# Hyena transforms at odd frequencies, with filters and inverse folded in halves and the value projection placed between their steps

## The chip, the cores and the metric

One core of a Trainium2 chip runs the whole program in a single launch. The metric is the device time in microseconds; three runs of the kernel before stand behind the median. The engines are named as in the profile: PE (TensorE matmuls), PEld (its weight loads), DVE (VectorE), ACT (ScalarE), POOL (GpSimd), SP (which issues the weight transfers).

## The reference

Two transformer blocks on 512 tokens of width 1024, all in float32. The change lies in the first mixer of the first block: two long convolutions over 512 positions, for 512 channels, with filters that a small network makes.

```python
def hyena_filters(L, ...):            # z: 33 features of each of the L times
    h = sin(freq[0] * (z @ w1 + b1)); h = sin(freq[1] * (h @ w2 + b2))
    h = (h @ w3).reshape(L, 2, ORDER, HY_W) * exp(-t * deltas)
    h_fwd, h_bwd = h[:, 0], h[:, 1]
    k2 = concatenate([h_fwd, zeros, h_bwd[1:][::-1]])     # length 2L
    return rfft(k2, axis=0)
def long_conv(z, kf, bias):
    zf = rfft(z, n=2 * L, axis=1)
    return irfft(zf * kf, n=2 * L, axis=1)[:, :L] + z * bias
def hyena_mixer(u, short_w, kf, bias):
    v, x1, x2 = split(dwconv3(u, short_w), 3)
    z = x1 * long_conv(v, kf[:, 0], bias[0])
    return x2 * long_conv(z, kf[:, 1], bias[1])
```

Beside it stand the input projection (`h @ w_in`, whose first 1536 columns feed this mixer and others the attention's queries, keys and values), neighbourhood attention, cross attention, two gated feed-forward networks and a second block. None of these is computed differently after the change.

## The kernel before

A float32 product is made of three passes: each operand is kept as a pair (hi, lo) of float32r tiles, and `mm` issues hi by hi, hi by lo and lo by hi, lines 370 to 372, each a matmul with a weight load of its own. The weights stream in as chunks of [128, 1024]: SP loads one into `raw` (4 buffers), ACT writes its hi part (line 299, `ws_h`), DVE subtracts to get the lo part (line 307, `ws_l`), into one of 3 split buffers. `chunk_act` and `chunk_dve` stand at fixed places in the two engines' programs and split up to two chunks beyond the one that PE is about to use, as far as buffers are free by then. All engines run their instructions in the order in which the functions issue them; semaphores alone tie them together. That order is written by hand: `hyena_pe`, `hyena_act`, `hyena_dve`, `hyena_pool`, then the same four for attention (`na_...`) and so on.

The Hyena part goes like this on PE. A tile `("hy", m)` is 8 blocks of the projection, 24 matmuls of 512 columns and one chunk; 12 of them make v, x1 and x2. A tile `("s", o, tt, i)` is 3 matmuls, and makes the sum (i = 0) or the difference (i = 1) of the forward and backward filter of order o at 128 times; DVE multiplies it by the decay (line 758), ACT makes the hi part (644), DVE the lo part (739, `mg_l`). `filters_pe(o)` transforms the four time tiles at frequencies 0 to 511 in four chunks (96 matmuls), and 12 more matmuls make the frequency 512 that an even transform also has. `long_conv_pe(o, src)` transposes the data (16 transposes), transforms it (96 matmuls, four chunks, results `zr`, `zi`), waits for the products with the filter, and transforms back (96 matmuls of 512 columns, four chunks, into four banks `("y", o, j)`). The products take four DVE multiplications from PSUM for each 128 frequencies (line 888), a subtraction and an addition on POOL (908), the hi parts on ACT (705, 708) and the lo parts on DVE (875). The whole for o = 0, then eight `s` tiles in a row (`HY2`), then the whole for o = 1. The banks come from a ring of seven. The eighth holds the totals of the norms.

In the hand-written order ACT and DVE finish a tile three steps behind its issue (`finish(HY1[n - 3])`), and DVE does a whole tile at once: scale, wait for ACT's middle tap, two side taps of the width-3 convolution (lines 748, 850, 853). After `("hy", 6)` DVE and ACT normalise the 16 meta tokens in 8 pairs of small operations each. `na_pe` starts with the value projection, `("V", m)`, four tiles of 24 matmuls, then the first query and key tiles, then the first scores.

## Time and profile before

| what | before |
|---|---|
| median of 3 runs | 2037.41 us (2033.86 to 2037.97) |
| the profiled execution | 2034.22 us, of which the span from first to last instruction is 2032.4 us |
| PE busy | 1885.5 us (93%), 9041 matmuls |
| DVE busy | 1013.8 us (50%) |
| ACT busy | 752.2 us (37%) |
| POOL busy | 273.2 us (13%) |
| mean granted TensorE clock | 0.962 |
| first matmul of the projection, last inverse matmul of o = 1 | 22.63 us, 270.66 us |
| first scores of the attention | 308.71 us |

Times inside the program are counted from the start of the span. A matmul's busy time in the profile is its latency: matmuls overlap, so the distance between the starts of two that follow each other (the pitch) is what one costs on PE. Idle time on PE is shown in brackets, with what ended it.

### The profile page before, as it was taken

How to read it: one execution, taken by the hardware profiler on the slowest of the kernel's cores; microseconds unless marked ns; L12 is line 12 of the kernel's file. 1: busy time of each engine (PE TensorE's matmuls, PEld its weight loads, DVE VectorE, ACT ScalarE, POOL GpSimd, SP SyncE). 2: the span in 40 equal slices, each digit the busy share in tenths (PEclk: the TensorE clock that was granted, in tenths of full speed). 3: DMA queues.
4: the chain of work that ended last, by engine and by line, in shares of the span. 5: the costliest groups of instructions: out<-in, count | busy, mean ns of one | idle time of the engine just before them, and what ended most of it. 6: DMA issues, size and time to landing. Idle time of an engine off the chain costs nothing. (4 is left out here: it accounts for less than half of the span.)

```text
span 2032.4 us, 22399 instructions
## 1 busy us (share of the span) xinstructions
PE 1885.5 (93%) x9041; PEld 1504.5 (74%) x9041; DVE 1013.8 (50%) x1510; ACT 752.2 (37%) x1248; POOL 273.2 (13%) x227
## 2 busy tenths in 40 slices
PE   5898999999999989889999999878967989999997
PEld 4776777678888877777888778766745668888886
DVE  6657554444354364445777722445454544444422
ACT  4343324432333443343434422325355533232221
POOL 1001200011211330042111100500000011111100
PEclk9998999999999999989999999888977999999998
DMA  5122232223223342122332232221220122222221
GB/s 177 63 94 73 83 114 84 73 82 106 83 93 102 137 145 73 34 70 78 99 104 83 83 104 94 93 84 42 90 73 16 36 82 84 94 93 94 94 93 52
DMA packets 49831, 175.35 MB, mean 86 GB/s; under 512 B 5883, under 2 KB 6523, under 8 KB 49601
## 3 DMA queue, kind: packets, MB, share of 16 engines
q1 hardware_dynamic: 45792, 160.41, 24.0%
q0 software_dynamic: 3936, 13.51, 1.9%
q8 instruction: 72, 1.18, 0.2%
q14 instruction: 31, 0.25, 0.0%
HBM read 169.70 MB, written 4.19 MB: 86 GB/s over the span
## 5 line engine op out<-in xcount | busy, mean ns | idle before, releaser
L307 DVE TENSOR_TENSOR ws_l<-raw,ws_h 128x1024 fp32r<-128x1024 f32 x297 | 401.1, 1354 | 587.2 <-ACT ws_h L299 586.7
L370 PE MATMUL ps<-h_h,ws_h 128*128 128x512 f32 (+1 forms) x1448 | 584.1, 403 | 42.7 <-DVE ws_l L307 23.3
L371 PE MATMUL ps<-h_l,ws_h 128*128 128x512 f32 (+1 forms) x1448 | 572.0, 395 | 0.0
L372 PE MATMUL ps<-h_h,ws_l 128*128 128x512 f32 (+1 forms) x1448 | 571.2, 395 | 0.0
L299 ACT ACTIVATE ws_h<-raw 128x1024 fp32r<-128x1024 f32 x297 | 312.2, 1055 | 489.9 <-PE ps L372 489.5
L370 PEld LDWEIGHTS ps<-h_h,ws_h 128*128 128x128 f32 x1448 | 278.3, 192 | 118.2 <-issue 22.9
L372 PEld LDWEIGHTS ps<-h_h,ws_l 128*128 128x128 f32 x1448 | 278.2, 192 | 61.6
L371 PEld LDWEIGHTS ps<-h_l,ws_h 128*128 128x128 f32 x1448 | 279.4, 193 | 59.0 <-issue 0.5
L370 PE MATMUL ps<-G_h,ws_h 128*128 128x512 f32 x352 | 139.8, 397 | 3.0 <-DVE ws_l L307 3.0
L372 PE MATMUL ps<-G_h,ws_l 128*128 128x512 f32 x352 | 139.7, 397 | 0.0
L371 PE MATMUL ps<-G_l,ws_h 128*128 128x512 f32 x352 | 139.6, 397 | 0.0
L414 POOL TENSOR_TENSOR sums<-sums,tmp 128x512 f32<-128x512 f32 (+2 forms) x48 | 53.7, 1119 | 494.3 <-ACT tmp L410 490.3
L370 PEld LDWEIGHTS ps<-G_h,ws_h 128*128 128x128 f32 x352 | 66.3, 188 | 19.7 <-DVE ws_l L307 3.5
L370 PE MATMUL ps<-mg_h,ws_h 128*128 128x512 f32 x200 | 79.5, 397 | 0.0
L371 PE MATMUL ps<-mg_l,ws_h 128*128 128x512 f32 x200 | 79.3, 396 | 0.0
L372 PE MATMUL ps<-mg_h,ws_l 128*128 128x512 f32 x200 | 79.2, 396 | 0.0
L371 PEld LDWEIGHTS ps<-G_l,ws_h 128*128 128x128 f32 x352 | 66.4, 189 | 16.3
L372 PEld LDWEIGHTS ps<-G_h,ws_l 128*128 128x128 f32 x352 | 66.4, 188 | 16.3
L370 PE MATMUL ps<-ya_h,ws_h 128*128 128x512 f32 (+1 forms) x160 | 58.1, 363 | 8.8 <-DVE ws_l L307 7.4
L1766 POOL TENSOR_TENSOR tmp<-tmp,tmp 128x512 f32<-128x512 f32 x22 | 35.2, 1600 | 210.7 <-DVE tmp L853 210.7
L1890 POOL TENSOR_TENSOR tmp<-tmp,tmp 128x512 f32<-128x512 f32 x22 | 28.7, 1306 | 225.4 <-ACT tmp L1839 190.3
L371 PE MATMUL ps<-ya_l,ws_h 128*128 128x512 f32 (+1 forms) x160 | 57.4, 359 | 0.0
(409 smaller groups left out, 2471.7 us busy)
## 6 DMA issues: line engine op xcount, KB each, us to landing
raw<-in_ffn_up SPq DMA_DIRECT2D x88, 512.0 KB, 3.4
raw<-in_w_merge SPq DMA_DIRECT2D x36, 512.0 KB, 3.4
raw<-in_ffn_down SPq DMA_DIRECT2D x22, 512.0 KB, 3.5
raw<-in_w_down SPq DMA_DIRECT2D x22, 512.0 KB, 3.4
raw<-in_fwd SPq DMA_DIRECT2D x16, 512.0 KB, 3.5
raw<-in_w_hy SPq DMA_DIRECT2D x12, 512.0 KB, 3.5
raw<-in_w_sc SPq DMA_DIRECT2D x12, 512.0 KB, 3.4
raw<-in_inv SPq DMA_DIRECT2D x8, 512.0 KB, 3.5
```

The lines of the kernel that those rows point to most:

```text
L299: act.e.activation(wsp[n % NSPLIT].hi, raw[n % NRAW][:], ACT.Copy).then_inc(*hi_made.says(("hi", n)))
L307: dve.e.tensor_tensor(w.lo, raw[n % NRAW][:], w.hi, ALU.subtract).then_inc(*lo_made.says(("lo", n)))
L370: pe.e.matmul(o, a.hi, b.hi, start=start, stop=False, skip_group_check=True)
L371: pe.e.matmul(o, a.hi, b.lo, start=False, stop=False, skip_group_check=True)
L372: return pe.e.matmul(o, a.lo, b.hi, start=False, stop=stop, skip_group_check=True)
L414: line.e.tensor_tensor(acc[:, 0:W], acc[:, 0:W], T[place.get(("sq", v, m), 0)][:, 0:W], ALU.add).then_inc(*sig.says(("added", v, m), ("gon ...
L1766: pool.e.tensor_tensor(u, u, v, ALU.mult).then_inc(*pool_part.says(("glu", i), ("gone", ("u", i, 1))))
L1890: pool.e.tensor_tensor(u, u, v, ALU.mult).then_inc(*pool_part.says(("glu2", i), ("gone", ("n8", i, 1))))
```

## The change

- The long convolutions are transformed at the 512 odd frequencies (2k + 1) of a doubled grid, not at 0 to 512. There is no separate last frequency, and no row 0 to mask (`row0`, `notrow0`, `KA` rows 8 and the DVE step on line 861 go).
- The 512 times are reordered, even ones first, in the filters' inputs and in the transposes (which now read the data with a step of two). Frequency k and 511 - k then have the same even part and the opposite odd part, up to sign. A filter transform `("F", o, q)` makes 128 + 128 frequencies from an even half and an odd half, 8 products of 3 matmuls, one chunk `fold`: 24 matmuls for 256 frequencies. ACT copies the even results out of PSUM, DVE makes sum and difference, four operations, into `KA` (`KA1` for o = 1).
- The data are transformed as before, in tiles `("Z", o, q, up)`, 24 matmuls and a chunk each. The products are written by DVE into `scr`, which lies in the space of `mg`.
- POOL now makes F and G of each Z tile (2 operations) and then, for each pair of Z tiles, the sums and differences of the two halves (4 operations, `("U", o, q)`), 8 for each q, 32 in all where there were 16. ACT and DVE split them into hi and lo as before.
- The inverse `("I", o)` works with 256 columns: even and odd times of the output are separate halves of a bank, two chunks, 96 matmuls of 256 columns.
- The order is one list, `HY_STEPS`, that PE, ACT and DVE all follow (`follow_steps`). Both orders' filters are made first, between the `hy` tiles. The last two `hy` tiles stand between the last Z tile of o = 0 and its inverse, and the four V tiles stand in the same way around the second convolution. DVE and ACT take up a tile one step after its issue; side taps and lo parts of the `s` tiles come one step later still.
- The banks come from one ring of eight. The meta tokens are normalised in one squaring, one reduction and two multiplications. The attention's biases of all four first heads are loaded only when the last inverse is done, since `y01` and `sums` now hold parts of the Hyena work.

On PE, at the head of the inverse of o = 0. Before (names: `ws` a weight chunk, `ya` the transposed data, `mg` the products KY), where the last matmuls of the transform of the data come right ahead:

```order
L371 MATMUL ps<-ya_l,ws_h 128x512
L372 MATMUL ps<-ya_h,ws_l 128x512
L370 MATMUL ps<-ws_h,mg_h 128x512
L371 MATMUL ps<-ws_l,mg_h 128x512
L372 MATMUL ps<-ws_h,mg_l 128x512
```

And after, where the last three matmuls of `("hy", 11)` come right ahead:

```order
L372 MATMUL ps<-h_h,ws_h 128x512
L373 MATMUL ps<-h_l,ws_h 128x512
L374 MATMUL ps<-h_h,ws_l 128x512
L372 MATMUL ps<-ws_h,mg_h 128x256
L373 MATMUL ps<-ws_l,mg_h 128x256
L374 MATMUL ps<-ws_h,mg_l 128x256
```

The number of inverse matmuls stays at 96 for each order. Their width goes from 512 to 256.

On POOL, the first Hyena operations. Before (behind the last sum for the meta tokens; all on four kept and two passing temporaries):

```order
L414 TENSOR_TENSOR sums<-sums,tmp_71 128x16
L908 TENSOR_TENSOR tmp_71<-tmp_71,tmp_75 128x512
L908 TENSOR_TENSOR tmp_72<-tmp_72,tmp_76 128x512
L908 TENSOR_TENSOR tmp_73<-tmp_73,tmp_75 128x512
L908 TENSOR_TENSOR tmp_74<-tmp_74,tmp_76 128x512
```

After (the four products of two Z tiles, then the folds into what ACT and DVE split):

```order
L888 TENSOR_TENSOR tmp_71<-scr_0_170,scr_1_171 128x512
L888 TENSOR_TENSOR tmp_72<-scr_2_172,scr_3_173 128x512
L888 TENSOR_TENSOR tmp_73<-scr_4_174,scr_5_175 128x512
L888 TENSOR_TENSOR tmp_74<-scr_6_176,scr_7_177 128x512
L888 TENSOR_TENSOR y_68<-tmp_71,tmp_73 128x512
L888 TENSOR_TENSOR tmp_71<-tmp_71,tmp_73 128x512
L888 TENSOR_TENSOR tmp_73<-tmp_72,tmp_74 128x512
L888 TENSOR_TENSOR tmp_72<-tmp_72,tmp_74 128x512
```

Four operations now stand for what were four, and four more follow them before ACT may start.

On DVE, around the split of the first chunk that the filter transform uses. Before (`ws_l` rows are the split chunks, 758 the decay, 739 the lo part, 748 the scaling of a `hy` tile):

```order
L748 TENSOR_TENSOR tmp_76<-ps,rh 128x512
L739 TENSOR_TENSOR mg_l<-tmp_74,mg_h 128x512
L850 SCALAR_TENSOR_TENSOR x_82<-tmp_76,par,x_82 128x511
L853 SCALAR_TENSOR_TENSOR x_82<-tmp_76,par,x_82 128x511
L758 TENSOR_TENSOR tmp_71<-ps,dec 128x512
L307 TENSOR_TENSOR ws_l<-raw_53,ws_h 128x1024
L307 TENSOR_TENSOR ws_l<-raw_54,ws_h 128x1024
```

And after (776 the decay, 842 the lo part, 770 the scaling, 873 and 876 the side taps):

```order
L842 TENSOR_TENSOR mg_l<-tmp_74,mg_h 128x512
L776 TENSOR_TENSOR tmp_71<-ps,dec 128x512
L873 SCALAR_TENSOR_TENSOR x<-tmp_75,par,x 128x511
L876 SCALAR_TENSOR_TENSOR x<-tmp_75,par,x 128x511
L776 TENSOR_TENSOR tmp_72<-ps,dec 128x512
L842 TENSOR_TENSOR mg_l<-tmp_71,mg_h 128x512
L776 TENSOR_TENSOR tmp_73<-ps,dec 128x512
L842 TENSOR_TENSOR mg_l<-tmp_72,mg_h 128x512
L309 TENSOR_TENSOR ws_l<-raw_56,ws_h 128x1024
L309 TENSOR_TENSOR ws_l<-raw_53,ws_h 128x1024
L776 TENSOR_TENSOR tmp_74<-ps,dec 128x512
```

The first of the two splits that follow each other is the chunk that `("F", 0, 0)` needs. It stands behind the operations of both groups of `s` tiles of o = 0.

The diff, cut to its core:

```diff
     def hyena_pe():
+        main = Ring(place, range(8))
...
+    HY_STEPS = ([("hy", m) for m in range(4)] + s_tiles(0, (0, 1)) + [("hy", 4)] + s_tiles(0, (2, 3)) + [
+        ("hy", 5), ("F", 0, 0), ("hy", 6), ("F", 0, 1)] + s_tiles(1, (0, 1)) + [("hy", 7)] + s_tiles(1, (2, 3)) + [
+        ("hy", 8), ("F", 1, 0), ("zT", 0), ("F", 1, 1), ("hy", 9), ("Z", 0, 0, 0), ("Z", 0, 0, 1), ("Z", 0, 1, 0),
+        ("Z", 0, 1, 1), ("U", 0, 0), ("hy", 10), ("U", 0, 1), ("hy", 11), ("I", 0), ("V", 0), ("V", 1), ("zT", 1),
+        ("Z", 1, 0, 0), ("Z", 1, 0, 1), ("Z", 1, 1, 0), ("Z", 1, 1, 1), ("U", 1, 0), ("V", 2), ("U", 1, 1), ("V", 3),
+        ("I", 1)])
...
+        def F(o, q):
+            n = chunk_pe("fold")
+            w = wsp[n % NSPLIT]
+            for odd in range(2):
+                for c in range(2):
+                    b = bank(("F", o, q, c, odd), main)
+                    for i in range(2):
+                        tt = 2 * odd + i
+                        pe.wait_ge(("sd", o, tt, c))
+                        last = mm(b, w[:, (4 * c + tt) * 128:(4 * c + tt + 1) * 128], (S_, D_)[c][:, tt, :], i == 0, i == 1)
+                last.then_inc(*products.says(("done", ("F", o, q, odd)), over(n) if odd else None))
...
+        def I(o):
+            ys = [bank(("y", o, j), main) for j in range(4)]
+            for q in range(2):
+                n = chunk_pe("inv")
+                w = wsp[n % NSPLIT]
+                for i in range(4):
+                    pe.wait_ge(("KY", o, 4 * q + i))
+                    for j, y in enumerate(ys):
+                        at = 256 * (i // 2)
+                        k = mm(y[:, at:at + 256], KY[:, 4 * q + i, j * 128:(j + 1) * 128], w[:, i * 256:(i + 1) * 256],
+                               q == 0 and i == 0, q == 1 and i % 2 == 1)
+                k.then_inc(*products.says(over(n), ("done", ("y", o, q))))
...
+    def follow_steps(chunk, begun, first, second):
+        for n, t in enumerate(HY_STEPS):
+            if t[0] in ("hy", "F", "Z", "V") or t[0] == "s" and t[2:] == (0, 0):
+                chunk()
+            elif t[0] == "I":
+                chunk()
+                chunk()
+            begun(t)
+            if n == 2:
+                first(HY_STEPS[0])
+            if n > 1:
+                first(HY_STEPS[n - 1])
+                second(HY_STEPS[n - 2])
...
     def hyena_pool():
+            for q in range(2):
+                for up in range(2):
+                    for i, (name, op) in enumerate((("F", ALU.subtract), ("G", ALU.add))):
+                        pool.wait_ge((a,) + t, (b,) + t, old)
+                        add(o, T[s][:, 0:L], scr[q][4 * up + 2 * i], scr[q][4 * up + 2 * i + 1], op, (name,) + t)
+                add(o, T[s][:, 0:L], at(Fa), at(Fb), ALU.add, u + (0,))
+                add(o, at(Fa), at(Fa), at(Fb), ALU.subtract, u + (2,))
+                add(o, at(Fb), at(Ga), at(Gb), ALU.subtract, u + (1,))
+                add(o, at(Ga), at(Ga), at(Gb), ALU.add, u + (3,), ("gone", Gb))
...
     def na_pe():
-        for m in range(4):
-            tile(bank(("V", m), vr), vblocks, 8, hk, ("V", m))
...
     def na_pool():
-            ready = ("neg", 4 * (hd // 2 - 2) + 3, hd % 2) if hd > 3 else ("sum", "meta") if hd == 1 else (
-                "done", ("y", 1, 3)) if hd > 1 else None
+            ready = ("neg", 4 * (hd // 2 - 2) + 3, hd % 2) if hd > 3 else ("done", ("y", 1, 1))
```

## Rows read from the trace of the kernel before

**Rows 1.** The page: span, busy time, granted TensorE clock in 40 slices
```profile
span 2032.4 us, 22399 instructions
...
PE 1885.5 (93%) x9041; PEld 1504.5 (74%) x9041; DVE 1013.8 (50%) x1510; ACT 752.2 (37%) x1248; POOL 273.2 (13%) x227
...
PEclk9998999999999999989999999888977999999998
```

**Rows 2.** Busy time by stretch: length, then busy and count by engine, clock, DMA
```profile
39.10:84.00 44.90, 42.62 (x184) 34.02 (x182) 30.52 (x47) 18.16 (x35) 2.33 (x7) 1.00 0.29 95
84.00:111.00 27.00, 22.71 (x88) 17.39 (x88) 21.55 (x31) 11.17 (x16) 0.00 (x0) 0.94 0.24 78
111.00:182.00 71.00, 70.27 (x310) 56.65 (x309) 39.71 (x47) 25.00 (x35) 12.51 (x8) 1.00 0.26 86
182.00:200.00 18.00, 12.90 (x38) 8.69 (x37) 15.50 (x24) 5.91 (x9) 0.00 (x0) 0.72 0.13 43
...
270.90:308.70 37.80, 35.59 (x161) 28.59 (x160) 20.85 (x27) 10.57 (x14) 1.07 (x2) 1.00 0.30 98
```

**Rows 3.** Waits of PE from 39 to 295 us: total, times, longest
```profile
PE ps L370 <- DVE x L809: 5.1, 4, 1.6
PE ps L370 <- DVE ws_l L307: 4.1, 2, 2.4
```

**Rows 4.** Timeline of PE: start, duration; 512 and 256 columns at both clocks
```profile
195.25 0.63 PE L371 MATMUL ps<-ws_l,HD_h 128*128 128x512 f32 x1
195.68 0.63 PE L372 MATMUL ps<-ws_h,HD_l 128*128 128x512 f32 x1
...
270.43 0.40 PE L371 MATMUL ps<-ws_l,mg_h 128*128 128x512 f32 x1
270.66 0.40 PE L372 MATMUL ps<-ws_h,mg_l 128*128 128x512 f32 x1
...
702.12 0.41 PE L370 MATMUL ps<-ya_h,ws_h 128*128 128x256 f32 x1
702.33 0.41 PE L371 MATMUL ps<-ya_l,ws_h 128*128 128x256 f32 x1
...
705.11 0.28 PE L372 MATMUL ps<-ya_h,ws_l 128*128 128x256 f32 x1
...
708.96 0.28 PE L372 MATMUL ps<-ya_h,ws_l 128*128 128x256 f32 x1
```

**Rows 5.** Timeline of DVE: the reciprocal, and two operations back to back
```profile
41.63 3.35 DVE L434 RECIPROCAL rh<-rh 128x512 f32<-128x512 f32 x1 [0.78 <-ACT rh L429]
...
94.65 0.68 DVE L739 TENSOR_TENSOR mg_l<-tmp,mg_h 128x512 fp32r<-128x512 f32 x1
95.25 0.68 DVE L758 TENSOR_TENSOR tmp<-ps,dec 128x512 f32<-128x512 f32 x1
```

**Rows 6.** Groups to 300 us, by shape: busy, mean ns, idle before
```profile
L299 ACT ACTIVATE ws_h<-raw 128x1024 fp32r<-128x1024 f32 x45 | 46.9, 1055 | 45.9 <-PE ps L372 45.8
...
L888 DVE TENSOR_TENSOR tmp<-ps,KA 128x512 f32<-128x512 f32 x32 | 19.8, 680 | 9.7 <-PE ps L372 9.7
...
L853 DVE SCALAR_TENSOR_TENSOR x<-tmp,par,x 128x511 f32<-128x511 f32 x12 | 9.0, 751 | 0.4
```

**Rows 7.** Timelines of DVE and POOL where both work, and DVE's splits
```profile
152.01 2.58 DVE L875 TENSOR_TENSOR mg_l<-tmp,mg_h 128x512 fp32r<-128x512 f32 x2
154.52 1.21 DVE L307 TENSOR_TENSOR ws_l<-raw,ws_h 128x1024 fp32r<-128x1024 f32 x1
...
717.29 2.28 DVE L307 TENSOR_TENSOR ws_l<-raw,ws_h 128x1024 fp32r<-128x1024 f32 x1
...
151.05 3.00 POOL L908 TENSOR_TENSOR tmp<-tmp,tmp 128x512 f32<-128x512 f32 x2 [2.07 <-DVE tmp L888]
...
722.02 10.32 POOL L414 TENSOR_TENSOR sums<-sums,sq 128x512 f32<-128x512 f32 x5
```

**Rows 8.** Timeline of PE: after the transposes, and the first scores
```profile
138.14 0.47 PE L370 MATMUL ps<-ya_h,ws_h 128*128 128x512 f32 x1 [0.73 <-DVE ya_l L868]
...
308.71 0.38 PE L1027 MATMUL ps<-mg_h 64*128 64x256 f32 x2 [0.52 <-DVE mg_l L1161]
```

More of the change, by code:

```diff
@@ new lines, in hy, with s @@
+            if m == 5:
+                total("meta", 16, bank(("sum", "meta"), main), 8, False)
+        chunk = {}
+        def s(o, tt, i):
+            if (tt, i) == (0, 0):
+                chunk["w3"] = chunk_pe("w3")
+            n = chunk["w3"]
+            b = bank(("s", o, tt, i), main)
+            pe.wait_ge(("H", i))
+            mm(b, (HS, HD)[i][:, tt * 128:(tt + 1) * 128], wsp[n % NSPLIT][:, o * 512:(o + 1) * 512], True, True).then_inc(
+                *products.says(("done", ("s", o, tt, i)), over(n) if (tt, i) == (3, 1) else None))
@@ new lines, in Z @@
+            for c in range(2):
+                b = bank(("Z", o, q, up, c), main)
+                for k in range(4):
+                    pe.wait_ge(("zt", o, k))
+                    i = mm(b, w[:, (4 * c + k) * 128:(4 * c + k + 1) * 128], zt[:, k, :], k == 0, k == 3)
+            i.then_inc(*products.says(over(n), ("done", ("Z", o, q, up))))
+        def I(o):
[10 more added lines that the diff above has]
+                k.then_inc(*products.says(over(n), ("done", ("y", o, q))))
@@ new lines, in V @@
+        def V(m):
+            tile(bank(("V", m), main), vblocks, 8, hk, ("V", m))
+        do = dict(hy=hy, s=s, F=F, zT=zT, Z=Z, I=I, V=V, U=lambda o, q: None)
+        for t in HY_STEPS:
+            do[t[0]](*t[1:])
+    def follow_steps(chunk, begun, first, second):
[11 more added lines that the diff above has]
+                second(HY_STEPS[n - 2])
+        first(HY_STEPS[-1])
+        second(HY_STEPS[-2])
+        second(HY_STEPS[-1])
@@ L719, in hyena_dve @@
+        follow_steps(chunk_act, begun, first, lambda t: None)
     def hyena_dve():
@@ new lines, in second @@
+        def second(t):
+            if t[0] == "hy":
+                m = t[1]
+                conv_sides(vx(m), t_slot(t)[:, 0:L], lambda q: P("hy_short", q * 12 + m), ("middle", t), ("side", t),
+                           ("v", 0, m), ("gone", t))
+            elif t[0] == "s":
+                _, o, tt, i = t
+                dst = (S_, D_)[i][:, tt, :]
+                dve.wait_ge(("f hi", t))
+                dve.e.tensor_tensor(dst.lo, t_slot(t)[:, 0:L], dst.hi, ALU.subtract).then_inc(
+                    *dve_part.says(("sd",) + t[1:], ("gone", t)))
@@ L824, in sine @@
+        follow_steps(chunk_dve, begun, first, second)
     def sine(b, n, i, bias, freq, slots):
@@ L1035, in V @@
                 pe.wait_ge(*(("scaled", ("V", m)) for m in range(4)))
-                transposes(b, [t_slot(("V", m))[:, 128 * tt:128 * tt + 128] for m in range(4)], ("done", ("Vt", tt)),
-                           *((("gone", ("V", m)) for m in range(4)) if tt == 3 else ()))
+                transposes(b, [vt(m)[:, 128 * tt:128 * tt + 128] for m in range(4)], ("done", ("Vt", tt)))
         def turn(t):
@@ L1147, in scaled @@
             return u
-        for m in range(4):
-            vblocks.next(8)
-            scaled(("V", m), kept)
         def project(p):
```

459 lines of the change are left out of this document (178 added, 281 removed).

## The prediction

> **What bounds the kernel now.** I read the page first: PE is busy 93% of a span of 2032.4 us, DVE 50%, POOL 13% [rows 1]. So time goes down either by fewer or shorter matmuls, or where PE waits. Then the stretches of the Hyena part, one row each, for the count of matmuls and the clock [rows 2], the list of PE's waits there [rows 3], and PE's timeline for what one matmul costs [rows 4]. At full clock a 512-column matmul starts 0.23 us after the one before (270.43 to 270.66; over 111 to 182 us, 294 of them besides 16 transposes, it comes to 0.233). At the low level of the clock, 1.2 GHz, it is 0.43 (195.25 to 195.68). A 256-column one takes 0.117 (33 of them from 705.11 to 708.96) and 0.21 at the low level (702.12 to 702.33) [rows 4]. So the busy time of a matmul, 0.40 or 0.28, is not what it costs.
>
> The two good stretches, such as 111 to 182 us, hold no waits worth naming. The bad ones are 84 to 111 us, 88 matmuls in 27.0 us where 88 x 0.233 = 20.5 would do, and 182 to 200, 38 in 18.0 us where 8.9 would do, at a clock of 0.72 [rows 2]. There the `s` tiles follow each other, and for each PE needs 0.7 us but DVE 1.2 (a decay and a lo part at a pitch of 0.60 [rows 5]). PE's own waits there are short (line 809, 1.6 us at most [rows 3]), and the halved clock behind them costs about as much again. With 2.3 us at 84 us and 0.73 at each data transform [rows 8], the Hyena part loses 6.5 + 9.1 + 2.3 + 1.5 = 19.4 us to waits and low clock after the first tiles.
>
> **The change on PE.** Filters: before 2 x (96 + 12) = 216 matmuls, after 4 F tiles of 24, so 120 fewer, 120 x 0.233 = 28.0 us. Inverse: 192 matmuls go from 0.233 to 0.117 [rows 4]: 22.3 us. Everything else on PE stays: 288 for `hy`, 48 for `s`, 192 for the data, 96 for V, 32 transposes. The transposes read the data with a step of two; no row shows that, and I bound it between nothing and a doubling of the 32 x 0.1 us that they take, so 0 to 3 us, and take 0, as only the 128-column weight load is strided. PE's work falls by 50.3 us. With all 19.4 us of loss gone too, 69.7 us would be the whole gain. What remains is which waits the new order has.
>
> **New waits, in order of time.** I lay DVE's list against PE's, with these prices: a split 1.14 (1.21 less the overlap), a PSUM or lo operation 0.60, the two side taps 1.5 [rows 5 to 7], a split on ACT 1.06 [rows 6].
>
> (1) The first filter transform. PE is free to begin it at 39.1 + 4 `hy` tiles x 5.6 + 8 `s` tiles x 0.7 = 67.1 us. DVE does the reciprocal first (3.35 us [rows 5], now behind one split, ending at 47.2) and then, before the split of the `fold` chunk is done: 5 scalings 3.0, 5 pairs of taps 7.9, 7 decays 4.2, 6 lo parts 3.6, 3 splits 3.4, some 1.0 of waiting for ACT: 23.1, hence 70.3 to 70.8. A wait of 3.6 us, and 0.9 more for the last lo part of the difference. 4.5 us, of which a lower clock behind it may cost 2 more (a clock of 0.94 over 27 us [rows 2] is 1.6).
>
> (2) The second group, eight `s` tiles with one `hy` tile between, then `F` for o = 1: the same list, but with an F and a `hy` tile of slack ahead, where DVE needs 4.1 and 3.2 us of PE's 5.6. I find it 1 us late.
>
> (3) The two stretches of Z tiles. Here DVE has per tile a split and four multiplications, 3.5 us of 5.6, and POOL 16 operations for each order. What one costs is between 1.3 (the shortest of its kind, estimated as 3.00 / 2 less the wait inside) and 2.06 (10.32 / 5, where DVE works beside it); 3.00 / 2 = 1.50 is the same operation in the same place [rows 7], and I take that. From the start of the first Z tile, the last 14 begin at +15.5 us (second Z tile done at 11.2, its products 1.6 to 2.4, a wait for DVE's split) and end at +36.5, then ACT's hi 0.6 and DVE's lo parts until about +39.5. PE needs the second half of the products at +39.1: four Z tiles 22.3, two `hy` tiles (or V2 and V3) 11.2, first half of the inverse 5.6. So the cover of 39.1 us is just enough. The products are asked for one by one over 5.6 us, so what is a little late costs little. At 2.06 the end is +47, 4 us late or more. At the same place DVE's split of the second inverse chunk is queued behind ACT's middle tap and four lo parts. I take 1.5 us for o = 0 and 1.0 for o = 1.
>
> What the row shows of DVE beside POOL: two lo parts take 2.58 us while POOL adds, 1.29 each, against a pitch of 0.60 alone, and a split takes 2.28 beside POOL's work and 1.21 alone [rows 5, 7]. I use these where they overlap. The Trainium skill, page "SBUF — State Buffer", section "Who interferes with whom", says that a DVE instruction with two SBUF inputs and a GpSimd instruction that reads SBUF block each other wholly, whoever starts first. By that rule six of DVE's operations and six of POOL's would stand strictly in turn, 13.7 us, and the second inverse chunk would be split at the moment when PE asks for it instead of 4 us before; the sum would rise by 0 to 2 us for each order. The 2.58 us agree with the rule, and so do the multiplications from PSUM, whose mean is 0.68 over all 32 [rows 6], as that of the decays alone [rows 5].
>
> (4) Data of o = 1: V0 and V1 (11.2 us) cover the 5.4 us in which DVE finishes the convolution; behind the transposes a wait of 1 us as before (0.73 [rows 8]). For o = 0 the F tile and a `hy` tile cover it: none.
>
> (5) The attention. Before, V's 22.3 us covered DVE's end of the convolution, and PE waited 0.52 us for the first scores [rows 8]. Now the query and key tiles, 11.2 us, come at once, and DVE has 8.6 us of work (12 operations) first, then two splits, two scalings and two lo parts. I reckon 2 us, 1.5 more than before. The biases, asked for only now, have 12 us to land. The other stages are unchanged, with the same waits.
>
> Chunks: 8 fewer, so DVE and ACT each lose 8 splits, off the path, and the transfers are not scarce.
>
> **The sum.** Work 50.3, old losses 19.4, new ones 4.5 + 2 + 1 + 1.5 + 1 + 1 + 1.5 = 12.5, which gives 57 us less: 2034.2 to 1977 for a profiled execution. The profiled one before stands 3.2 us below the median of its runs, 2037.41. I put the median after between the two readings: 1979.
>
> **Rivals.** (A) No new wait lasts: 3 us in all, gain 67, 1970. For it speaks that the first wait hangs on one reckoning of DVE's list. (B) POOL is the bound of both Z stretches: at 2.06 us an operation, with DVE's splits queued behind it, PE waits 4 to 8 us for each order and the clock falls behind each wait, 5 us more for each. Gain 57 less 17 to 24, so 1996 to 2003. For it speaks that DVE and POOL would each be busy over three quarters of a stretch where before POOL was busy for 12.5 of 71 us [rows 2]; against it, the 1.50 in the same place. (C) The other side, the clock. The new order has a short wait ahead of nearly every step, and if the engine is held at 1.2 GHz a 512-column matmul costs 0.43 instead of 0.233. Before, it fell so after waits of about 1.6 and 1.6 us with 6 matmuls between (0.72 over 18 us [rows 2, 3]). The gain of 57 us is gone when some 290 of the 720 matmuls of 512 columns that are left run so, 125 us at the low level, since each costs 0.197 more; with 400 of them the time is 1979 + 79 = 2058. Against it: wherever PE had 0.7 us of wait or less between tiles the clock stayed at 1.00 (111 to 182 us [rows 2]). (D) The halves don't shorten the inverse, if 256 columns were held up by strided output or by the weight load, 22 us less gain, 2001. The matmuls at 705 us had a weight load each and ran at 0.117 [rows 4], so this is nearly shut out.
>
> **Chances.** Forecast 0.60, A 0.15, B 0.18, C 0.02, D and the like 0.05. The range is from 1966 (A, and a low reading) to 1999 (most of B); C and the rest are left out. The likeliest case alone: 1970 to 1988. About 0.2%, 4 us, is what the measurement can tell from no change. Faster 0.97, same 0.01, slower 0.02.
>
> **What would show it.** PE: 120 matmuls fewer; inverse matmuls at a pitch of 0.12; a bracket of 3 to 4 us before the first F tile, named after DVE's split, and small ones at the second inverse chunk of each order; the first scores at about 252 us instead of 308.7. POOL: 32 additions with a mean near 1.5. Wrong it would be by a mean over 2, by brackets of many us named after POOL's or ACT's hi of the products, or by a clock under 0.9 in the Hyena part.

## The result

| what | before | after |
|---|---|---|
| median | 2035.63 us (4 runs, 2032.52 to 2037.97) | 1969.93 us (4 runs, 1965.65 to 1978.72) |
| ratio | | 0.9684, 95% interval 0.9646 to 0.9721 |
| profiled execution | 2034.22 us, span 2032.4 us | 1965.65 us, span 1963.9 us |
| first projection matmul to first scores | 286.08 us (22.63 to 308.71) | 225.49 us (21.79 to 247.28) |
| from the first scores to the end of the span | 1723.7 us | 1716.6 us |

A second profile of the same kernel, with five timed rounds, gave 1977.15 us against 2040.8, ratio 0.9684 (0.9661 to 0.9706). The change is worth 3.2%, and the prediction of 1979 us (1966 to 1999) was right in sign and nearly in size: 9 us too high beside the first median. Between the two profiles of the table, 60.6 us come from the stretch that the change rewrites and 7.1 from behind it. The second figure is no firm one: in the ten profiles of the kernel after and of the versions of it below, bank3 left out, the time from the first scores to the end lies anywhere from 1716.0 us (hy_early) to 1733.2 us (hy_before_f).

The page of the kernel after, to be held against [rows 1]:

```profile
span 1963.9 us, 22095 instructions
PE 1831.5 (93%) x8921; PEld 1468.3 (75%) x8921; DVE 1015.5 (52%) x1504; ACT 734.2 (37%) x1216; POOL 295.7 (15%) x236
PEclk9999999999999899999999999889987989999998
```

There are 120 matmuls fewer, as reckoned. PE's busy share is 93% as before: its busy time fell by 54.0 us, its idle time from 146.9 to 132.4. Next, PE's timeline in the kernel after: every start in the Hyena part and at the attention's head with a wait of over 0.4 us, behind the first tiles (it answers [rows 3, 8]), with the transposes of o = 1.

```profile
69.21 0.74 PE L372 MATMUL ps<-mg_h,ws_h 128*128 128x512 f32 x1 [3.58 <-DVE ws_l L309]
106.45 0.50 PE L372 MATMUL ps<-mg_h,ws_h 128*128 128x512 f32 x1 [1.87 <-DVE ws_l L309]
182.92 2.07 PE L393 MATMUL ps<-ident,x 128*128 128x128 f32 x16
186.24 0.47 PE L372 MATMUL ps<-ya_h,ws_h 128*128 128x512 f32 x1 [1.25 <-DVE ya_l L791]
233.60 0.51 PE L372 MATMUL ps<-h_h,ws_h 128*128 128x512 f32 x1 [2.16 <-DVE x L807]
247.28 0.39 PE L1027 MATMUL ps<-mg_h 64*128 64x256 f32 x2 [0.52 <-DVE mg_l L1154]
```

The two rows that answer [rows 2] around the filters, the window of each order's POOL work, and the first inverse on PE (its first two and its last matmul, then the next tile's first):

```profile
67.00:90.00 23.00, 20.79 (x82) 16.64 (x83) 14.86 (x21) 10.47 (x15) 0.00 (x0) 0.93 0.35 115
90.00:115.00 25.00, 23.13 (x98) 18.55 (x97) 21.03 (x32) 11.33 (x17) 0.00 (x0) 0.93 0.25 85
...
136.30:165.10 28.80, 28.80 (x146) 24.09 (x145) 25.50 (x26) 8.50 (x12) 25.27 (x16) 1.00 0.23 73
195.80:224.50 28.70, 28.70 (x144) 23.95 (x143) 24.55 (x25) 8.23 (x11) 25.17 (x16) 1.00 0.27 89
```

```profile
160.35 0.28 PE L372 MATMUL ps<-ws_h,mg_h 128*128 128x256 f32 x1
...
171.60 0.28 PE L374 MATMUL ps<-ws_h,mg_l 128*128 128x256 f32 x1
171.72 0.39 PE L372 MATMUL ps<-h_h,ws_h 128*128 128x512 f32 x1
```

The 96 matmuls of the inverse run from 160.35 to 171.72, 0.118 each, without one wait between them. In the first window beside POOL, PE is busy without a break, DVE for 25.5 us of 28.8 and POOL for 25.3: three engines are nearly full at once, and PE waits for neither of the others.

### The profile page after: what moved, and what is told of

The parts are those of the page before. It is cut to its first block and busy times, and to the rows that moved or that the text cites. A ratio compares the mean times of both kernels' runs of the same rounds, so it can differ in the third digit from the quotient of the medians.

```text
span 1963.9 us, 22095 instructions
## 1 busy us (share of the span) xinstructions
PE 1831.5 (93%) x8921; PEld 1468.3 (75%) x8921; DVE 1015.5 (52%) x1504; ACT 734.2 (37%) x1216; POOL 295.7 (15%) x236
## 5 line engine op out<-in xcount | busy, mean ns | idle before, releaser
L309 DVE TENSOR_TENSOR ws_l<-raw,ws_h 128x1024 fp32r<-128x1024 f32 x289 | 393.1, 1364 | 577.1 <-ACT ws_h L301 576.8
L301 ACT ACTIVATE ws_h<-raw 128x1024 fp32r<-128x1024 f32 x289 | 303.9, 1055 | 504.9 <-PE ps L374 504.6
L373 PEld LDWEIGHTS ps<-h_l,ws_h 128*128 128x128 f32 x1448 | 279.0, 193 | 59.1 <-issue 0.5
L416 POOL TENSOR_TENSOR sums<-sums,tmp 128x512 f32<-128x512 f32 (+1 forms) x41 | 51.6, 1259 | 455.8 <-ACT tmp L412 453.0
L374 PEld LDWEIGHTS ps<-G_h,ws_l 128*128 128x128 f32 x352 | 66.0, 187 | 16.3
L372 PE MATMUL ps<-mg_h,ws_h 128*128 128x512 f32 x160 | 64.7, 405 | 5.4 <-DVE ws_l L309 5.4
L373 PE MATMUL ps<-mg_l,ws_h 128*128 128x512 f32 x160 | 64.5, 403 | 0.0
L374 PE MATMUL ps<-mg_h,ws_l 128*128 128x512 f32 x160 | 64.4, 402 | 0.0
L374 PE MATMUL ps<-ya_h,ws_l 128*128 128x512 f32 (+1 forms) x160 | 57.5, 359 | 0.0
```

What stands on the lines that cost most here:

```text
L301: act.e.activation(wsp[n % NSPLIT].hi, raw[n % NRAW][:], ACT.Copy).then_inc(*hi_made.says(("hi", n)))
L309: dve.e.tensor_tensor(w.lo, raw[n % NRAW][:], w.hi, ALU.subtract).then_inc(*lo_made.says(("lo", n)))
L372: pe.e.matmul(o, a.hi, b.hi, start=start, stop=False, skip_group_check=True)
L373: pe.e.matmul(o, a.hi, b.lo, start=False, stop=False, skip_group_check=True)
L374: return pe.e.matmul(o, a.lo, b.hi, start=False, stop=stop, skip_group_check=True)
L416: line.e.tensor_tensor(acc[:, 0:W], acc[:, 0:W], T[place.get(("sq", v, m), 0)][:, 0:W], ALU.add).then_inc(*sig.says(("added", v, m), ("gon ...
```

## Experiments

Each is told by what it tells apart. "The distance" is the time from the first projection matmul to the first scores in its profile, 225.49 us in the kernel after. Its second profile has 227.48, with a clock of 0.94 in one window of 30 us (210 to 240) where the first has 1.00, behind the same wait of 2.16 us: some 2 us are noise of the clock. The stretch from the first projection matmul to the first F tile, the same program in all versions that leave it alone, takes from 47.4 to 48.5 us (pool_more), so another 1 us of the distance is noise.

### The terms of PE's work: fold_more and inv512

Thirty matmuls more in each F tile (54, where there are 24):

```diff
-                        last = mm(b, w[...], (S_, D_)[c][:, tt, :], i == 0, i == 1)
+                        for again in range(2 if c or i else 3):
+                            last = mm(b, wt, st, i == 0 and again == 0, i == 1)
```

> The kernel after with 30 matmuls more in each of the four F tiles (54 instead of 24: as many as the unfolded filters had, 216 in all; some of them are accumulated several times, so the filters' spectra are wrong). It measures the term 'filters, 120 x 0.233 = 28.0 us'. Theory 1: TensorE alone sets the time: 28 us more than the kernel after. Theory 2: part of what the fold saved went into the waits for the splits around it: DVE catches up during the longer F tiles, the waits of 1.9 us before F of the second order and the low clock behind go, and it costs only 22 to 26 us more.

```profile
70.84 0.50 PE L372 MATMUL ps<-mg_h,ws_h 128*128 128x512 f32 x1 [3.59 <-DVE ws_l L309]
...
85.09 0.40 PE L372 MATMUL ps<-h_h,ws_h 128*128 128x512 f32 x1
```

The F tile takes 14.25 us here, from its first start to that of the `hy` tile behind it, and 7.26 in the kernel after; the four tiles together take 28.0 us more, as reckoned. The distance is 253.76 us, 28.3 more; the ratio to before is 0.9835 (0.9804 to 0.9867). Theory 1. The waits of 3.59 and 1.88 us before the F tiles stand unchanged, so longer F tiles do not help DVE to be in time.

The inverse with 512 columns instead of 256:

```diff
-                        at = 256 * (i // 2)
-                        k = mm(y[:, at:at + 256], KY[...], w[:, i * 256:(i + 1) * 256], ...)
+                        at = 512 * (i // 2)
+                        k = mm(y, KY[...], w[:, at:at + 512], ...)
```

> The kernel after with the same 192 inverse matmuls at 512 columns each instead of 256 (the inverse is then computed wrongly: each takes both halves of the chunk). It measures the term 'inverse, 22.3 us' of the sum. Theory 1: the inverse is bound by TensorE alone, each matmul goes from 0.117 to 0.233, 22.3 us more than the kernel after: ratio to it 1.011. Theory 2: the halves hung on the products of POOL and DVE (no slack), so that with 512 columns part of the 22.3 us only fills what would have been waits: 10 to 20 us more.

```profile
162.50 0.40 PE L372 MATMUL ps<-ws_h,mg_h 128*128 128x512 f32 x1
...
184.90 0.40 PE L372 MATMUL ps<-h_h,ws_h 128*128 128x512 f32 x1
```

The first inverse takes 22.40 us from its first start to the next tile's, where the kernel after has 11.37, and the second grows by as much: 22.1 us for both, against 22.3 reckoned. The distance is 249.34 us, 23.9 more. The 1.8 us that it has beyond are 1.0 before the first F tile (noise, as said), a clock of 0.91 over 250 to 270 us (1.8), and against them a clock of 1.00 over 90 to 115 us where the kernel after has 0.93 (1.75 less, with a wait of 0.65 us for a lo part showing in its place). The ratio is 0.9813 (0.9783 to 0.9843). The listed waits are those of the kernel after to 0.01 us, so nothing of the 22 us had been bought with a wait for POOL or DVE. Theory 1 again.

### The work alone in the old order: old_order_less_work

```diff
-            for k in range(4):
+            for k in range(2):
...
-                    k = mm(y, KY[...], w[:, i * 512:(i + 1) * 512], ...)
+                    k = mm(y[:, 256 * i:256 * i + 256], KY[...], w[:, i * 512:i * 512 + 256], ...)
```

> The kernel before, in its order and on its banks, with the change's saving of matmuls alone: filter transforms with two of four time tiles each (102 matmuls instead of 216, 114 x 0.233 = 26.6 us) and inverse matmuls at 256 columns (192 x 0.116 = 22.3 us); half of the filters' times and half of the inverse's frequencies are left out, so the output is another. Theory 1: work alone, and the order gave the rest: 48.9 us less than the kernel before, waits as there. Theory 2: without the new order the saved work turns into waits for DVE's products and splits (the Z and U tiles stood apart), so 25 to 45 us less. The kernel after is 64 us less.

The distance is 245.92 us, 40.2 less than before's 286.08, where 48.9 us of work are gone. Ratio 0.9795 (0.9763 to 0.9828), 40.7 us by the medians. Theory 2: 8.7 us did not come, mostly turned into waits and low clock. Its timeline and windows of PE:

```profile
156.82 0.39 PE L370 MATMUL ps<-ws_h,mg_h 128*128 128x256 f32 x1 [2.61 <-DVE ws_l L307]
...
223.99 0.58 PE L370 MATMUL ps<-ws_h,mg_h 128*128 128x256 f32 x1 [2.56 <-DVE ws_l L307]
```

```profile
84.00:111.00 27.00, 22.13 (x85) 16.92 (x86) 21.49 (x31) 10.76 (x15) 0.00 (x0) 0.94 0.23 77
165.00:190.00 25.00, 19.75 (x64) 14.04 (x65) 19.77 (x30) 12.75 (x19) 0.00 (x0) 0.80 0.22 68
```

The first window is as bad as it was before [rows 2], and so is the row of `s` tiles in the second. In either inverse a new wait of 2.6 us has come: with halved matmuls PE asks for the next chunk earlier than DVE can split it. The kernel after does 1.4 us less work than this one and is 20.4 us shorter in the distance. 19 us are the order's, with all that belongs to it, and that is more than the order: this run still splits 44 chunks in the distance, where the kernel after splits 36, and the two new waits (5.2 us) stand in inverses that use four chunks each instead of two. The order with the old chunks, or the old order with the new ones, was not run, so how the 19 us divide is not shown.

### What the order covers: hy_early, v_after, pool_more

The last two `hy` tiles ahead of the Z tiles of o = 0:

```diff
-        ... ("hy", 9), ("Z", 0, 0, 0), ... ("Z", 0, 1, 1), ("U", 0, 0), ("hy", 10), ("U", 0, 1), ("hy", 11), ("I", 0),
+        ... ("hy", 9), ("hy", 10), ("hy", 11), ("Z", 0, 0, 0), ... ("Z", 0, 1, 1), ("U", 0, 0), ("U", 0, 1), ("I", 0),
```

> The kernel after with the last two hy tiles (11.2 us) ahead of the four Z tiles of o = 0, so that they no longer stand between these and the first inverse. Same work. It measures the slack of POOL's and DVE's chain at the first inverse. Theory 1: the last products are ready only 0.6 to 3 us before TensorE asks for them, so 8 to 10.6 us of wait appear in the first inverse. Theory 2: the chain's end is itself set by the order (POOL starts on the last products when DVE and the banks let it), so it moves forward with them and 0 to 5 us appear.

```profile
163.83 0.36 PE L372 MATMUL ps<-ws_h,mg_h 128*128 128x256 f32 x1 [3.70 <-DVE mg_l L825]
167.10 0.58 PE L372 MATMUL ps<-ws_h,mg_h 128*128 128x256 f32 x1 [0.81 <-DVE mg_l L825]
176.64 0.36 PE L372 MATMUL ps<-ws_h,mg_h 128*128 128x256 f32 x1 [3.20 <-DVE mg_l L825]
```

```profile
165.00:190.00 25.00, 20.99 (x118) 19.34 (x117) 14.37 (x16) 4.42 (x7) 9.58 (x6) 0.81 0.19 64
```

Taking 11.2 us of cover away brings 7.7 us of wait, a little under what theory 1 expected (8 to 10.6), and far over theory 2. So the chain had 3.5 us to spare, not nothing. The clock falls to 0.81 behind the waits, and the distance grows by 14.0 us, or 12.0 beside the second profile of the kernel after: 1.6 to 1.8 times the waits. The ratio is 0.9713 (0.9689 to 0.9737).

The V tiles behind the second inverse:

```diff
-        ("I", 0), ("V", 0), ("V", 1), ("zT", 1), ... ("U", 1, 0), ("V", 2), ("U", 1, 1), ("V", 3), ("I", 1)])
+        ("I", 0), ("zT", 1), ... ("U", 1, 0), ("U", 1, 1), ("I", 1), ("V", 0), ("V", 1), ("V", 2), ("V", 3)])
```

> The kernel after with the four V tiles of the value projection (22.4 us of TensorE work) put back behind the second inverse, where the kernel before had them. Theory 1, by DVE's and POOL's lists: V0 and V1 cover the 5.4 us in which DVE ends the first convolution, V2 and V3 give 11.2 of the 39 us that POOL and DVE need for the second order's products. Without them TensorE waits about 5 us at the data transposes of o = 1 and 8 to 11 us in the second inverse, and the 2.2 us before the first query tile go: 12 to 16 us later at the first scores than the kernel after (225.5 us from the first projection matmul), with a clock under 1.00 behind the waits. Theory 2: POOL runs far enough ahead, so only the 5 us come, less 2: 3 us later.

```profile
178.73 3.66 PE L393 MATMUL ps<-ident,x 128*128 128x128 f32 x16 [5.32 <-DVE x L813]
...
208.87 0.55 PE L372 MATMUL ps<-ws_h,mg_h 128*128 128x256 f32 x1 [3.30 <-DVE mg_l L825]
...
221.69 0.55 PE L372 MATMUL ps<-ws_h,mg_h 128*128 128x256 f32 x1 [3.88 <-DVE mg_l L825]
```

5.3 us at the transposes, 7.6 in the second inverse (a wait of 0.38 lies between the two shown), and the 2.2 before the first query tile are gone: 10.7 us of waits on balance, 16.3 us in the distance, with a clock of 0.86 in the two windows 165 to 190 us and 210 to 240 us. The ratio is 0.9753 (0.9728 to 0.9778). Theory 1, with a little less wait in the inverse than its 8 to 11; the placing of V between the steps is worth 14 to 16 us of the 65.

Each of POOL's additions for F and G twice:

```diff
+                        add(o, T[s][:, 0:L], scr[q][4 * up + 2 * i], scr[q][4 * up + 2 * i + 1], op, ("first", name) + t)
+                        pool.wait_ge(("first", name) + t)
                         add(o, T[s][:, 0:L], scr[q][4 * up + 2 * i], scr[q][4 * up + 2 * i + 1], op, (name,) + t)
```

> The kernel after with each addition of the filters' unfolding on POOL done twice (the same sum into the same place): 16 additions more for each order, 32 in all, of 1.3 us alone and 1.7 beside DVE. Theory 1 (POOL just fits into its cover, the forecast's place for rival B): those of them that stand in POOL's chain ahead of the last products, about half of the 16, at 1.3 to 1.7 us less the slack of 0.6 to 3, show as a wait in each inverse: 8 to 12 us for each order, 16 to 24 in all. Theory 2 (POOL is off the path by far, since it idles while TensorE does the next tile): under 5 us in all.

The expectation counts them wrongly: F and G make 8 additions for each order, so 8 were added for each, 16 in all, not 16 and 32. The waits are 6.06 and 0.38 us in the first inverse, 5.24 and 0.38 in the second:

```profile
173.02 0.55 PE L372 MATMUL ps<-ws_h,mg_h 128*128 128x256 f32 x1 [6.06 <-DVE mg_l L825]
...
240.59 0.55 PE L372 MATMUL ps<-ws_h,mg_h 128*128 128x256 f32 x1 [5.24 <-DVE mg_l L825]
```

```profile
165.00:190.00 25.00, 18.56 (x103) 16.45 (x102) 16.09 (x19) 7.16 (x9) 10.31 (x8) 0.86 0.24 84
240.00:260.00 20.00, 16.88 (x78) 14.69 (x79) 16.59 (x22) 7.33 (x11) 5.37 (x6) 0.76 0.37 116
```

The four waits make 12.1 us, under the 16 to 24 of theory 1, which had counted twice the additions, and far over the 5 of theory 2; the distance grows by 19.2 us, and the ratio is 0.975 (0.9722 to 0.9779). Theory 1: POOL stands right behind the path, and rival B named the right place. By the 3.5 us of hy_early, some four microseconds more of POOL for the first order would have made it the bound (an estimate).

### The waits before the filter transforms: hy_before_f, early_split, early_split_o0

First a `hy` tile more ahead of the F tiles of either order:

```diff
-        ("hy", 5), ("F", 0, 0), ("hy", 6), ("F", 0, 1)] + s_tiles(1, (0, 1)) + [("hy", 7)] + ...
+        ("hy", 5), ("hy", 6), ("F", 0, 0), ("hy", 7), ("F", 0, 1)] + s_tiles(1, (0, 1)) + [("hy", 8)] + ...
```

> The changed kernel with one more projection tile ahead of the first filter transform of each order (hy 6 before F of order 0, hy 9 before F of order 1), all else in the same order. Theory 1: the waits of 3.58 us at 69 us and of 1.87 us at 106 us come from DVE's list, which is late by the work of the s tiles, and 5.6 us more of PE's work cover them. Then both brackets go, with the stretch at the low clock behind each, and the time is 6 to 9 us below the changed kernel. Theory 2: DVE is the bound of this whole stretch (busy 25.3 of 27.9 us), and the waits only move to the tiles behind. Then the gain is under 3 us and brackets show up later, before the first Z tile.

```profile
70.22 0.47 PE L372 MATMUL ps<-h_h,ws_h 128*128 128x512 f32 x1 [3.69 <-DVE ws_l L309]
...
112.99 0.50 PE L372 MATMUL ps<-mg_h,ws_h 128*128 128x512 f32 x1 [1.86 <-DVE ws_l L309]
```

The wait of 3.6 us did not go, it moved to the `hy` tile that now stands there. The distance (226.99) and the ratio (0.968, 0.9656 to 0.9705) are those of the kernel after, so theory 2 has the gain right; but no new wait shows up further on, the old two stay. So it is not a wait for the filters: it is the next chunk, whatever it holds. In the kernel after, ACT and DVE do this at the second place:

```profile
104.10 1.99 ACT L301 ACTIVATE ws_h<-raw 128x1024 fp32r<-128x1024 f32 x2
```

```profile
103.44 0.68 DVE L842 TENSOR_TENSOR mg_l<-tmp,mg_h 128x512 fp32r<-128x512 f32 x1
105.17 2.36 DVE L309 TENSOR_TENSOR ws_l<-raw,ws_h 128x1024 fp32r<-128x1024 f32 x2 [1.05 <-ACT ws_h L301]
```

Two chunks are split back to back at the end of DVE's list for the eight `s` tiles. DVE is not busy right before them: it idles 1.05 us here, and 1.04 at the first place (67.93 us), until ACT has split its half, and ACT has that behind the hi part of an `s` tile, which waits for DVE's decay. By the program there are two reasons why they come no earlier: the chunk of the `s` tiles holds one of the three split buffers while a `hy` tile stands between them, and the place of the split in both engines' programs is behind that tile's decay. Only the second was tested. The next version has the tile order of hy_before_f, puts the split ahead of the last `s` tile's follow-up, and moves the first attention head to other banks (cut; the ring of its value tiles moves too):

```diff
+            if t[0] == "s" and t[2:] == (2, 1):
+                early()
...
-        bs, b1, bT, bO = Ring(place, (0, 1)), Ring(place, (2, 3)), Ring(place, (4, 5)), Ring(place, (6, 7))
+        bs, b1, bT, bO = Ring(place, (0, 1)), Ring(place, (4, 5)), Ring(place, (2, 3)), Ring(place, (6, 7))
```

> The kernel after, with three edits: one hy tile more ahead of the F tiles of either order, the split of the next weight chunk put ahead of the last s tile's follow-up on ACT and DVE, and other banks for the first attention head (so that its query tile does not land on the banks the convolution still holds). Theory 1: the 3.6 us before the first F tile, the 1.9 before that of the second order and the 2.2 before the first query tile go, and with the first two the lower clock behind them (0.93 over 50 us, 3.5 us): 5 to 10 us less than the kernel after, 1964 to 1972 beside 1977. Theory 2: DVE has more work than TensorE has up to there, so the wait only moves to another tile (as it did when only the hy tile was moved): within 2 us of the kernel after, and a wait of 3 us or more stands somewhere between 60 and 115 us.

```profile
113.42 0.50 PE L372 MATMUL ps<-mg_h,ws_h 128*128 128x512 f32 x1 [1.94 <-DVE mg_l L844]
...
116.89 0.49 PE L372 MATMUL ps<-mg_h,ws_h 128*128 128x512 f32 x1 [1.80 <-DVE mg_l L844]
```

The distance is 221.81, 3.7 less; the ratio is 0.9663 (0.9633 to 0.9692), 1966.56 us. Both theories had a part. At o = 0 the wait of 3.6 us is gone and one of 0.99 stands at 79.08 us, for a lo part; at o = 1 two waits for lo parts came, which the earlier split pushed back on DVE. The clock is 1.00 in both windows. So the last version splits early for the first order alone:

```diff
-            if t[0] == "s" and t[2:] == (2, 1):
+            if t[0] == "s" and t[1:] == (0, 2, 1):
```

> The last version (hy tile moved, earlier split, other attention banks), but with the earlier split for the first order alone: in the second order the earlier split stood on DVE ahead of lo parts that TensorE wanted, and 1.94 and 1.80 us of waits took the place of 1.9. Theory 1: one wait of 1.9 us before the F tile of o = 1 is back and those two are gone: 1.5 to 2.5 us less than the last version at the first scores (219.5 to 220.5 us from the first projection matmul, instead of 221.8). Theory 2: the two waits come from the tile order, not the split, and stay: 221.8 to 224. In the whole time, 1962 to 1970 beside 1977 for the kernel after; the intervals of the two can overlap.

```profile
67.00:90.00 23.00, 21.71 (x93) 16.90 (x92) 18.86 (x28) 9.70 (x15) 0.00 (x0) 1.00 0.31 111
90.00:115.00 25.00, 22.53 (x96) 17.56 (x94) 20.91 (x30) 11.89 (x17) 0.00 (x0) 1.00 0.27 87
...
109.23 0.50 PE L372 MATMUL ps<-mg_h,ws_h 128*128 128x512 f32 x1 [1.87 <-DVE ws_l L309]
...
242.40 0.39 PE L1029 MATMUL ps<-mg_h 64*128 64x256 f32 x2 [1.50 <-DVE mg_l L1156]
```

The distance is 219.76, 5.7 less than in the kernel after and inside theory 1's 219.5 to 220.5. Gone are 3.6 us of wait, 3.4 of low clock in the same two windows (1.00 where 0.93 stood) and 1.2 at the attention's head; new are waits of 0.99 and 0.64 us for lo parts, at 78.46 and 115.04. That makes 6.6, so 0.9 us of it did not reach the distance. Of the low clock only the first half can be called the version's. The second stands behind the wait of 1.87 us, which is still here, and pool_more, whose program is that of the kernel after up to there, has this wait with a clock of 1.00 behind it too:

```profile
107.84 0.50 PE L372 MATMUL ps<-mg_h,ws_h 128*128 128x512 f32 x1 [1.87 <-DVE ws_l L309]
...
113.65 0.50 PE L372 MATMUL ps<-mg_h,ws_h 128*128 128x512 f32 x1 [0.65 <-DVE mg_l L842]
```

The ratio is 0.965 (0.9626 to 0.9673), 1967.03 us. It is the best of the versions, by its distance and by its ratio, though its interval overlaps that of the kernel after. The three edits were never run singly: which of them took the first wait away is read from the place of the split, not shown alone.

### The stages that the change does not touch: bank3, before_bank0, after_again

Before, PE waited at the head of the merge stage; after, the wait is gone. The row of the kernel before, and that of bank3 (below):

```profile
450.14 0.50 PE L370 MATMUL ps<-h_h,ws_h 128*128 128x512 f32 x1 [3.53 <-DVE tmp L1138]
```

```profile
392.12 0.50 PE L372 MATMUL ps<-h_h,ws_h 128*128 128x512 f32 x1 [3.53 <-DVE tmp L1135]
```

The merge stage takes its banks from the ring of seven that the Hyena part used before. Eighty Hyena tiles leave it at bank 3, which the last tile of the stage ahead still holds. After, the Hyena part has a ring of its own and the ring of seven starts at bank 0. The two experiments set the start by hand, in the kernel after to bank 3, in the kernel before to bank 0:

```diff
+        rings["main"].n = 3
```

```diff
+        main.n = 0
```

> The changed kernel once more, to have it beside the others on the same chip. Its four runs so far lay between 1965.65 and 1978.72 us, the kernel before between 2032.52 and 2037.97. I expect a ratio to the kernel before of 0.965 to 0.971, and the first scores of the attention at 247 us in its profile.

> The changed kernel, where only the ring of seven PSUM banks that the merge stage and later stages use starts at bank 3, as it did before the change, and not at bank 0. Theory 1: the wait of 3.53 us that PE had before at 450 us is a wait for bank 3, which the last short-convolution tile still held, and it went only because the change takes the Hyena part's tiles out of this ring. Then the wait of 3.5 us is back right behind the attention's last tiles, and the time is 3.5 us above that of the changed kernel, or up to 7 where the later stages' smaller waits (66.1 against 69 us of distance between the two kernels' traces) hang on the same count. Theory 2: that wait went for another reason, such as the loads of the biases or the earlier end of the value projection. Then the trace shows no wait there and the time is that of the changed kernel within 1 us.

> The kernel before, where only the ring of seven banks is set back to bank 0 at the start of the merge stage. Theory 1 (the bank): the bracket of 3.53 us at 450 us goes, and the time is 3.5 to 7 us below the kernel before, a ratio of 0.9965 to 0.998. Theory 2 (something else in the change): no difference, 1.000 within 0.001.

| kernel | ring starts at | ratio to before | waits of PE over 0.8 us behind 310 us, summed |
|---|---|---|---|
| before | 3 | 1 | 92.8 us |
| bank3 | 3 | 0.9703 (0.968 to 0.9726) | 91.5 us |
| before_bank0 | 0 | 0.9947 (0.9927 to 0.9966) | 85.8 us |
| after | 0 | 0.9684 (0.9646 to 0.9721) | 84.5 us |
| after_again | 0 | 0.9684 (0.9661 to 0.9706) | 84.5 us |

Setting the start of the ring takes 7.0 us of these waits out of either kernel, but not all of that is the bank's. Two waits go with it in every profile: the 3.53 us shown, and one before scores in the second block (`ps<-KN_h,QN_h`, at 1390 us in the kernel before). The three profiles that start at bank 3 (before, bank3, old_order_less_work) have 3.53 and 2.2 us there, the eleven that start at 0 have none and 0.94 to 0.96. That is 4.8 us. The rest also moves where the bank does not: a wait of 5.0 us that becomes 4.3 in the pairs is 5.0 in fold_more and v_after too, with bank 0, and one of 4.9 that becomes 4.0 is 4.0 in old_order_less_work, with bank 3. Over all profiles the sum of the last column is 91.5 to 92.8 with bank 3 and 84.5 to 90.1 with bank 0. Which bank the second wait collides with was not followed. In whole times, before_bank0 gained 10.8 us by its ratio (7 to 15), more than theory 1's 3.5 to 7, and some 6 us of that have no row; bank3 lost 3.9 (its interval and that of after_again overlap). So the cause of the two waits is shown, and of the 7.1 us behind the first scores in the table of the result it explains 4.8.

## Why the prediction was right or wrong

| part of the sum | predicted | measured |
|---|---|---|
| filters, 120 matmuls | 28.0 us | 28.0 (fold_more, on the F tiles) |
| inverse, 256 columns | 22.3 us | 22.1 (inv512, on the inverses) |
| transposes with a step | 0, 0 to 3 | 0.3 (16 in 2.07 us, before 1.91; twice) |
| old losses | 19.4 us | 21.5 (waits 14.9; low clock 6.6, as 0.94 over 27 us and 0.72 over 18): the sum left out a wait of 1.71 us for a split at 283.91 us, in the V tiles, the second of the two in [rows 3] |
| (1) before the first F tile | 4.5 + 2 low clock | 3.58 + 1.6 low clock (0.93 over 23 us) |
| (2) before F of o = 1 | 1 | 1.87 + 1.75 low clock (0.93 over 25 us) |
| (3) POOL's cover, both orders | 2.5 | 0 |
| (4) data of o = 1 | 1 | 1.25 |
| (5) attention's head | 1.5 more | 2.16, at the first query tile and not at the first scores (0.52 as before) |
| everything behind | nothing | 4.8 less by the banks, 7.1 less in the profiles of the table |

**Right.** PE's work, 50.1 us of the 50.3, and that nearly nothing of it would be lost to new waits. Counting matmuls by pitch, and not by busy time, gave it: 0.40 us of busy time each would have made 48 us of the filters alone. The first wait was reckoned from DVE's list at 3.6 us and came as 3.58, in part by luck: PE was free at 65.6 us and not 67.1, the split done at 69.2 and not 70.3 to 70.8, so both ends were off by over a microsecond the same way. The 0.9 us more for the last lo part did not come. Its cause was told too narrowly, as a backlog of DVE alone: hy_before_f gave 5.6 us of cover and could not take it away, and DVE idles 1.04 us for ACT right before the split, so the place of the split in both lists belongs to the cause.

**The new waits** add up to 12.2 us where 12.5 were forecast, but only because errors cancel. Term (3) was the largest single mistake among them. The step that failed is "the cover of 39.1 us is just enough", turned into 2.5 us. POOL's operations took 25.27 / 16 = 1.58 us, near the 1.50 taken, and its end came at 165.1 us, 38.3 us behind the first Z tile's start (126.8) and not 36.5. Yet nobody waited. The last two lo parts begin at 166.17 and end at 167.45, 40.7 us behind that start and later than the +39.5 reckoned, while PE asks for the four products of the second half at 166.0, 167.4, 168.9 and 170.3. The prediction says that "what is a little late costs little", and then gave it 1.5 and 1 us. hy_early measures what the spare time was in the first order: 3.5 us.

**Term (5)** failed in its place. The wait for the first scores was to grow. What grew was a wait 13.7 us earlier: the first query tile needs a bank that the convolution's last result still holds (`x L807`, 2.16 us). Only DVE's list was followed, not who frees the bank. In early_split, with other banks, that wait is gone and 1.50 stands at the scores, where 2.0 had been forecast.

**The step that failed most** is the sentence "the other stages are unchanged, with the same waits". Their instructions are unchanged. Their banks are not, since the ring's position is handed on from the Hyena part, and two waits of 4.8 us go with it. The diff shows it, in the `main` ring of eight that the Hyena part now makes for itself.

The distance fell by 60.6 us: 50.1 for work less 0.3 for transposes, 21.5 less 12.2 for waits and clock, which is 59.1; 1.5 us are left without a row. With the 7.1 behind it and the first projection matmul 0.8 us sooner, that is the 68.5 us between the two profiled spans; the medians differ by 65.7.

**The rivals.** (A), that no new wait lasts, named 1970 us, the very time measured, and its mechanism is not what happened: 8.9 us of new waits and 3.4 of low clock stand in the trace. The time came from the old wait left out, the unspent 2.5 and the stages behind; part of the agreement is luck of the run, since the second median is 1977.15. (B), POOL as the bound, did not come about at 1.58 us an operation, but pool_more shows how near it was. (C), the held clock: 0.93 in two windows, 1.00 elsewhere in the first profile. (D), halves that don't shorten: shut out by 0.118 us a matmul and by inv512.

**DVE beside POOL.** In the kernel after, POOL and DVE stand against each other as follows (two timelines, POOL's then DVE's):

```profile
151.14 1.30 POOL L888 TENSOR_TENSOR y<-scr,scr 128x512 f32<-128x512 f32 x1
...
156.35 1.74 POOL L888 TENSOR_TENSOR KA<-scr,scr 128x512 f32<-128x512 f32 x1
158.05 1.74 POOL L888 TENSOR_TENSOR tmp<-y,sums 128x512 f32<-128x512 f32 x1
```

```profile
149.59 2.47 DVE L800 TENSOR_TENSOR scr<-ps,KA 128x512 f32<-128x512 f32 x4
...
155.16 5.17 DVE L825 TENSOR_TENSOR mg_l<-tmp,mg_h 128x512 fp32r<-128x512 f32 x3
...
163.87 1.78 DVE L825 TENSOR_TENSOR mg_l<-tmp,mg_h 128x512 fp32r<-128x512 f32 x1
...
166.17 1.28 DVE L825 TENSOR_TENSOR mg_l<-sums,mg_h 128x512 fp32r<-128x512 f32 x2
```

A lo part, both inputs in SBUF, costs DVE 0.60 us from start to start when POOL is still (the last row) and 1.70 beside it (5.17 less the overlap of 0.08, over 3), and POOL's addition takes 1.74 instead of 1.30: the two alternate, one of each in 1.70 us. Multiplications that read PSUM keep 0.60 (2.47 for four, at 149.59) in the same stretch. The Trainium skill, page "SBUF — State Buffer", section "Who interferes with whom", says that such a pair blocks each other wholly, and the rows agree but for some 0.2 us: 0.60 and 1.30 make 1.90. Six of each would take 10.2 us at this pace and not the 13.7 of the prediction. The time that the prediction gave it, 0 to 2 us for each order, came out as 0, since the lo parts had the room.

## What to carry to other kernels

Where PE is busy 93% of the time, cutting its work pays in full only if the order gives the engines behind it their time: here much the same cut was worth 40 us in the old order and 60 in the new one (with fewer chunks to split besides). Lay the other engines' lists against PE's tile by tile, ask of every tile who frees its bank and its buffer, and price waits with the clock that may fall behind them. And where a ring of banks or buffers is shared between stages, count its position at the hand-over on both sides of a change: a stage that is not edited can still change its waits.

## What was not expected of the hardware

- A stretch with waits costs more than the waits, 1.3 to 1.8 times as much. hy_early has 7.7 us of waits and is 14.0 us longer, pool_more 12.1 and 19.2, v_after 10.7 on balance and 16.3 (2 us less each beside the second profile of the kernel after), with a granted clock of 0.76 to 0.86 in the windows with and behind the waits.
- Behind a single wait of some 2 us the clock is not settled by the program. The same 1.87 us before the F tile of o = 1 has 0.93 over 90 to 115 us in both profiles of the kernel after and 1.00 in pool_more and inv512; the same 2.16 us before the first query tile has 1.00 behind it in one profile of the kernel after and 0.94 over 30 us in the other.
- DVE and POOL in turn cost DVE nearly three times the price of the operation (0.60 to 1.70 us), while POOL loses only a third (1.30 to 1.74).
- Transposes that read SBUF with a step of two cost 0.16 us more for sixteen.
